# A gate and up step pair that takes the last quarter of the inner dimension two steps later

## The reference, cut to what matters

```
h = h + concatenate([oa, ob, oc, od], axis=-1) @ w_out[i]
y = _rms(h, norm_ffn_g[i])                    # y = h / sqrt(mean(h^2) + eps) * g
h = h + (silu(y @ w_gate[i]) * (y @ w_up[i])) @ w_down[i]
```

## Time and profile before

| | us |
|---|---|
| median of three runs (2075.77 to 2077.26) | 2076.1 |
| time of the profiled execution | 2075.89 |
| its span | 2074.0 |
| TensorE busy | 2054.3 (99%) |
| VectorE busy | 1533.5 (74%) |
| ScalarE busy | 1039.4 (50%) |
| mean granted clock | 0.998 |

### The profile page before, as it was taken

The page is one execution under the profiler, slowest core; times in us unless marked ns, Lnnn a source line. Parts: engine busy times, 40 slices in busy tenths (PEclk is TensorE's granted clock), DMA queues, the critical chain, the costliest instruction groups (busy, mean ns, idle before and its releaser), DMA issues.

```text
span 2074.0 us, 24910 instructions
## 1 busy us (share of the span) xinstructions
PE 2054.3 (99%) x10391; PEld 1746.8 (84%) x10391; DVE 1533.5 (74%) x1421; ACT 1039.4 (50%) x982; POOL 21.1 (1%) x40
## 2 busy tenths in 40 slices
PE   9999999999999999999999999999999999999998
PEld 8888888888888888888999987888888888888887
DVE  6576554665688888856789869978788787887565
ACT  6444444544455555545344446545455464555453
POOL 2000000000000000000000000000000000000000
PEclk9999999999999999999999999999999999999999
DMA  8655555555566655665655555746557465556462
GB/s 250 215 181 182 163 163 184 173 174 193 170 223 203 223 203 183 203 223 183 206 185 163 184 202 197 255 143 215 190 203 243 159 218 172 190 175 223 153 235 80
DMA packets 224735, 398.35 MB, mean 192 GB/s; under 512 B 11202, under 2 KB 56506, under 8 KB 224368
## 3 DMA queue, kind: packets, MB, share of 16 engines
q1 hardware_dynamic: 221344, 387.64, 56.2%
q0 software_dynamic: 2528, 8.00, 1.3%
q10 hardware_dynamic: 752, 1.12, 0.2%
HBM read 394.62 MB, written 2.12 MB: 191 GB/s over the span
## 4 chain that ended last, share of the span: by engine, by line
PE 91%; DVE 6%; ACT 1%; DMA 1%; issue 1%; ACTq 0%; SPq 0%; DVEq 0%
PE psA L679 22%; PE psA L681 21%; PE psA L680 21%; PE psA L885 6%; PE psB L679 4%; PE psB L680 4%; PE psB L681 4%; PE psA L889 3%; DVE lo L1678 2%; DVE CA L1967 1%; PE psB L943 1%; DVE raw L1695 1%; ACT hi L1216 1%; DMA X<-in_x_dram 0%; DMA raw<-in_w_up_dram 0%
## 5 line engine op out<-in xcount | busy, mean ns | idle before, releaser
L1678 DVE TENSOR_TENSOR lo<-raw,hi 128x2048 fp32r<-128x2048 f32 (+2 forms) x373 | 843.3, 2269 | 289.5 <-ACT hi L1216 287.6
L1216 ACT ACTIVATE hi<-raw 128x2048 fp32r<-128x2048 f32 (+2 forms) x373 | 706.7, 1900 | 468.6 <-PE psA L681 314.4
L679 PE MATMUL psA<-hi,XHL 128*128 128x512 f32 (+1 forms) x1048 | 409.4, 391 | 3.1 <-DVE XHL L1775 1.7
L681 PE MATMUL psA<-hi,XHL 128*128 128x512 f32 (+1 forms) x1048 | 406.5, 388 | 0.0
L680 PE MATMUL psA<-lo,XHL 128*128 128x512 f32 (+1 forms) x928 | 359.5, 387 | 0.0
L679 PE MATMUL psA<-hi,YHL 128*128 128x512 f32 x624 | 244.4, 392 | 0.0
L681 PE MATMUL psA<-hi,YHL 128*128 128x512 f32 x624 | 243.0, 389 | 0.0
L679 PEld LDWEIGHTS psA<-hi,XHL 128*128 128x128 f32 x1048 | 196.9, 188 | 44.3 <-DVE lo L1678 2.2
L681 PEld LDWEIGHTS psA<-hi,XHL 128*128 128x128 f32 x1048 | 196.7, 188 | 40.7
L680 PE MATMUL psA<-lo,YHL 128*128 128x512 f32 x576 | 224.1, 389 | 0.0
L680 PEld LDWEIGHTS psA<-lo,XHL 128*128 128x128 f32 x928 | 174.4, 188 | 34.5
(11 more groups left out here) (427 smaller groups left out, 2708.9 us busy)
## 6 DMA issues: line engine op xcount, KB each, us to landing
raw<-in_w_in_dram SPq DMA_DIRECT2D x149, 1024.0 KB, 5.1
raw<-in_w_down_dram SPq DMA_DIRECT2D x37, 1024.0 KB, 5.2
raw<-in_w_up_dram SPq DMA_DIRECT2D x35, 1024.0 KB, 5.2
raw<-in_w_gate_dram SPq DMA_DIRECT2D x35, 1024.0 KB, 5.2
raw<-in_w_out_dram SPq DMA_DIRECT2D x32, 1024.0 KB, 5.1
raw<-in_w_ple_gate_dram SPq DMA_DIRECT2D x16, 1024.0 KB, 5.1
raw<-in_w_branch_dram SPq DMA_DIRECT2D x13, 1024.0 KB, 5.1
raw in Y<-in_w_in_dram SPq DMA_DIRECT2D x9, 1024.0 KB, 5.1
```

The lines of the kernel that those rows point to most:

```text
L679: e.matmul(dst, A2[0], B2[0], start=first, stop=False, skip_group_check=True)
L681: return e.matmul(dst, A2[1], B2[0], start=False, stop=last, skip_group_check=True)
L1216: e.activation(hi[u % H][:, 0:m], raw[slot][:, 0:m], ACT.Copy).then_inc(hi_made, 1)
L1678: e.tensor_tensor(lo[slot][:, 0:m], raw[slot][:, 0:m], hi[u % H][:, 0:m].bitcast(F32), ALU.subtract).then_inc(lo_made, 1)
```

## The change: what it does

For S 0 alone the steps get another order, `START`: a, x, p2, f, e, d, p3, p0, c, g, p1. Step p3, the one that uses the last quarter of the activations in the gate product, moves from the fifth to the seventh place; e and d move up. The other ten step groups and the six of the first layer keep `STEPS`.

With it the turn of the last quarter moves by one unit, from ahead of p2 (238) to ahead of f (239), on all three engines. Its squares move on ScalarE from the end of unit 235 to the end of unit 236, behind the copy P1. The norm's root moves on VectorE from unit 239 to 241. Form e (the difference d - b, which takes b's buffer) is made behind the low part of f, where it was made ahead of that of p3. All sums of `gate_up` that stood at steps d and p0 stand at p0. Step d no longer closes quarter C; p3 does. In `fills` S 0 walks `FILLED_EARLY`, in which c comes ahead of p3.

```diff
@@ -64,6 +64,7 @@
 MIX_ORDER = (0, 3, 2, 1)
 
 STEPS = ("a", "x", "p2", "f", "p3", "e", "d", "p0", "c", "g", "p1")
+START = ("a", "x", "p2", "f", "e", "d", "p3", "p0", "c", "g", "p1")
 SOURCE = {"a": (0, 0), "b": (1, 0), "c": (0, 4), "d": (1, 4), "p0": (0, 8), "p1": (0, 12), "p2": (1, 8), "p3": (1, 12)}
 FILLED = ("a", "b", "x", "d", "p2", "f", "p3", "c", "g", "p0", "p1")
 FILLED_EARLY = ("a", "b", "x", "d", "p2", "f", "c", "p3", "g", "p0", "p1")
@@ -100,7 +101,7 @@
         group(("branch", 4 * b + f), "N", A["w_branch"][0, b], 512 * f, [[(k, 4 * b + k) for k in range(4)]])
 
     def mixed(name, W, cols, banks):
-        g = Group(len(groups), name, "S", W, cols, STEPS, len(units))
+        g = Group(len(groups), name, "S", W, cols, START if name == ("S", 0) else STEPS, len(units))
         g.banks = banks
         groups.append(g)
         for i in range(len(STEPS)):
@@ -221,8 +222,8 @@
         if g.kind == "S":
             if i:
                 continue
-            for role in FILLED_EARLY if g.name[0] == "gs" else FILLED:
-                until = u + STEPS.index("e" if role == "b" else role)
+            for role in FILLED_EARLY if g.name[0] == "gs" or g.parts == START else FILLED:
+                until = u + g.parts.index("e" if role == "b" else role)
                 if role in SOURCE:
                     n, k0 = SOURCE[role]
                     take(u, (g.name, role), until, g.W[n], k0, 4, [(g.cols[n], 512)])
@@ -457,7 +458,7 @@
             g, i = units[u]
             if g.kind != "S":
                 return places[u]
-            role = STEPS[i]
+            role = g.parts[i]
             return places[g.name, "b" if role == "e" else role]
 
         def block_of(j):
@@ -543,8 +544,8 @@
         LAST_GATES = named["gs", GATES - 1].first
         MERGE = {LAST_GATES + 3: 0, LAST_GATES + 5: 1, OUT: 2, OUT + 1: 3}
         TURN1 = {OUT + 6 + 4 * f: f for f in range(4)}
-        TURN2 = {OUT2 + 6 + 4 * f: f for f in range(4)}
         BEGIN = [named["S", j].first for j in range(11)]
+        TURN2 = {OUT2 + 6: 0, OUT2 + 10: 1, OUT2 + 14: 2, BEGIN[0] + 3: 3}
         TURN3 = {named["down", 16 + f].last + 2: f for f in range(4)}
         TURNH = {BEGIN[j + 1] + 3: j for j in (0, 2, 4, 6, 8, 9)}
         TURNH |= {named["down", 2 * j - 2].first + 1: j for j in (1, 3, 5, 7)}
@@ -801,7 +802,7 @@
 
             def mixed(u):
                 g, i = units[u]
-                role, j = STEPS[i], g.name[1]
+                role, j = g.parts[i], g.name[1]
                 early = g.name[0] == "gs"
                 free = gates_free if early else mixed_free
                 FH, FL = (GSFH, GSFL) if early else (SFH, SFL)
@@ -844,12 +845,12 @@
                     if j == 0 and not early:
                         e.wait_ge(flip_low, SECOND + 4)
                     block("D", 12, t1, last=True)
-                    x = block("C", 12, t0)
+                    x = block("C", 12, t0, last=g.parts == START)
                 elif role == "e":
                     e.wait_ge(*copied(g, "U2"))
                     x = form("A", 3)
                 elif role == "d":
-                    x = form("C", 4, last=True)
+                    x = form("C", 4, last=g.parts == STEPS)
                 elif role == "p0":
                     free(j, "B")
                     block("B", 8, t0, first=True)
@@ -1207,8 +1208,8 @@
                 g, i = units[u]
                 m = UNIT if g.kind == "S" else g.width * len(g.parts[i])
                 slot, _, landed = place(u)
-                if g.kind == "S" and STEPS[i] in FORMS:
-                    e.wait_ge(form_made, 4 * order(g) + FORMS[STEPS[i]])
+                if g.kind == "S" and g.parts[i] in FORMS:
+                    e.wait_ge(form_made, 4 * order(g) + FORMS[g.parts[i]])
                 else:
                     e.wait_ge(raw_landed[slot], landed)
                 if u >= H:
@@ -1554,7 +1555,7 @@
                 elif name == "bg":
                     e.wait_ge(bank_dve, g.freed)
                     part_high(c4(B[:, 3, :]), 1, 1.0)
-                elif name == "out2":
+                elif name == "out2" and n < 3:
                     e.wait_ge(bank_dve, g.freed)
                     squares(n, X, ss3, ss3_made)
                 elif name == "down" and n >= 16:
@@ -1593,7 +1594,7 @@
             for u in range(n_units):
                 g, i = units[u]
                 side(u)
-                if g.kind == "S" and STEPS[i] == "x":
+                if g.kind == "S" and g.parts[i] == "x":
                     mixed(u)
                 if 0 < u < n_units - AHEAD and u not in ATTEND and u not in EARLY:
                     split(u + AHEAD)
@@ -1606,10 +1607,13 @@
                 if u in ENDED and ENDED[u].name[0] == "gs":
                     first_gates(ENDED[u])
                 if g.kind == "S":
-                    if STEPS[i] != "x":
+                    if g.parts[i] != "x":
                         mixed(u)
                 elif u == g.last:
                     post(g)
+                if u == BEGIN[0]:
+                    e.wait_ge(bank_dve, freed(("out2", 3)))
+                    squares(3, X, ss3, ss3_made)
             e.wait_ge(ple_sum, 6)
             for m, (t, c, n) in enumerate(LAST):
                 ts = slice(512 * t + c, 512 * t + c + n)
@@ -1681,7 +1685,7 @@
             def mixed(u):
 
                 g, i = units[u]
-                role, j = STEPS[i], order(g)
+                role, j = g.parts[i], order(g)
                 of = {r: raw[places[g.name, r][0]][:, :] for r in FILLED}
 
                 def arrived(r):
@@ -1706,26 +1710,28 @@
                     arrived("c")
                     e.wait_ge(form_made, 4 * j + 2)
                     form("g", "c", "f")
-                elif role == "p3":
+                elif role == "p3" and g.parts == STEPS:
                     form("b", "d", "b")
                 split(u)
+                if role == "f" and g.parts == START:
+                    form("b", "d", "b")
 
             def gate_up(u):
 
                 g, i = units[u]
-                role, j = STEPS[i], g.name[1]
+                role, j = g.parts[i], g.name[1]
                 early = g.name[0] == "gs"
                 third, sums0, sums1 = (GSU3, GCG[:, 0:512], GCG[:, 512:1024]) if early else (SU3, CG1, CG2)
-                if role == "d":
+                if role == ("p0" if g.parts == START else "d"):
                     e.wait_ge(*copied(g, "U3"))
                     finish(e.tensor_tensor(sums1, sums1, third[:, :], ALU.add))
-                    e.wait_ge(unit_done, g.first + STEPS.index("p3") + 1)
+                    e.wait_ge(unit_done, g.first + g.parts.index("p3") + 1)
                     e.tensor_tensor(sums1, sums1, quarter(g, "D"), ALU.add).then_inc(gate_made, 1)
-                elif role == "p0":
-                    e.wait_ge(unit_done, g.first + STEPS.index("d") + 1)
+                if role == "p0":
+                    e.wait_ge(unit_done, g.first + max(g.parts.index("d"), g.parts.index("p3")) + 1)
                     e.wait_ge(*copied(g, "U2"))
                     e.tensor_tensor(sums0, sums0, quarter(g, "C"), ALU.add).then_inc(gate_made, 1)
-                elif role == "g" and not early:
+                if role == "g" and not early:
                     e.wait_ge(fg_tanh, j + 1)
                     e.scalar_tensor_tensor(out=CG[:, :], in0=THF[:, :], scalar=1.0, in1=CG[:, :], op0=ALU.add,
                                            op1=ALU.mult).then_inc(gate_made, 1)
@@ -2136,7 +2142,7 @@
                 if u in TURN2:
                     f = TURN2[u]
                     low(SECOND + f, XL[:, 4 * f:4 * f + 4, :], XH[:, 4 * f:4 * f + 4, :], 1, scale_cols(32, f))
-                if u == BEGIN[0] + 3:
+                if u == BEGIN[0] + 5:
                     e.wait_ge(ss3_made, 4)
                     row_sums(ss3, v2)
                     mean_eps(v2, 2048)
```

## The result

The changed kernel takes 2080.94 us (median of 15 runs, 2079.73 to 2081.95), the kernel before beside it 2076.83 (15 runs, 2075.77 to 2077.74): a ratio of 1.0021, interval 1.0014 to 1.0027, slower by 4.1 us. The profiled execution took 2081.48 us, with a span of 2079.7 against 2074.0. Three single executions of the experiments (7370.93 us in experiment 7, 2275.57 us in experiment 4, 5349.89 us of the kernel before) lie far outside all others, and the ratios leave them out.

A forecast was written before the change was run, and what follows sets the result against it. TensorE's own matmuls, 91% of the chain that ended last, were taken to bound the kernel. A stall of +2.4 us and a clock loss of +1.5 us summed to 3.9 us, giving 2080.0 us, range 2077.0 to 2082.2.

The forecast's parts named there:

- the line of 4.15 us: Whole kernel: change below 0.2% can't be told from none; chances 0.60 same, 0.37 slower, 0.03 faster.
- The early high part of f, the early copy of C, no wait ahead of p2: ScalarE makes f's high part about 1256.4, copies C at 1263.55; p2 starts right behind x at 1261.30.
- The chain to copy U2: ScalarE's copy of f's sum stands behind four pieces, the first waiting for form e; e starts about 1276.3.
- The stall's term, +2.4 us: Between f and e TensorE stands still 5.5 to 6 us, so e starts 2.4 us late against 1273.87.
- The clock's term, +1.5 us: The long stall ahead of e halves TensorE's clock; half of 2.9 us of slow matmuls is lost.
- The upper bound of 2.9 us: Largest clock loss behind the stall, if full clock is given back later than at the kernel's start.
- The root, the gate sums, the turn's place, the loads: nothing: Moved VectorE work, the moved turn and reordered weight loads were expected to add no new wait.
- the second wait: Rival, 0.10: later gate sums push VectorE past its slack in the second half-pair; about 2081.5 us.
- The stall without clock loss: Rival, 0.20: TensorE stalls ahead of e but its clock doesn't fall; 2078.5 us.
- The copy in time: Rival, 0.08: ScalarE copies right behind f, e waits about 1.1 us, starts at 1271.5; 2073.7 us.
- The useful part of the change: Up to the end of f: the step after could start at 1270.35 instead of 1273.87, gaining 3.5 us.

The follow-up runs named there:

- experiment 7: Kernel before, with only the last quarter's squares moved to the end of unit 236 on ScalarE: 2075.56 us, ratio 0.9996.
- experiment 4: Changed kernel with 22 unused matmuls between f and e, ahead of all waits of e: 2078.59 us, ratio 1.0009.
- Experiments 1: Changed kernel with ScalarE's copy U2 ahead of p3's high part instead of behind it: 2078.75 us, ratio 1.0011.
- experiment 8: Changed kernel with the last quarter's turn back at unit 238 and the root back at unit 239: 2081.38 us, ratio 1.0023.
- experiment 2: Changed kernel with copy U2 at the head of f's iteration, also ahead of the turned quarter's high part: 2076.74 us, ratio 1.0001.
- experiment 6: Changed kernel with copy U2 at the head of f's iteration and form e ahead of f's low part: 2075.54 us, ratio 0.9996.
- experiment 3: Changed kernel with 20 unused matmuls between f and e, behind the wait for e's low part: 2081.06 us, ratio 1.0020.

## Why the prediction was right, point by point

The forecast was 2080.0 us, the measured time 2080.94, inside the range. The loss is 4.1 us where 3.9 were forecast; the rest of the difference is the kernel before, which stands at 2076.83 over 15 runs against 2076.1 over three. That 3.9 lies so near to 4.1 is partly luck: of the two terms one came out 0.5 us smaller by the times and the other 0.7 us larger. And the loss lies right at the line of 4.15 us that the forecast drew between "same" (0.60) and "slower" (0.37); on which side it fell was not foreseen. With 15 runs of each kernel it is clear of the spread.

- *The early high part of f, the early copy of C, no wait ahead of p2*: right. They stand at 1256.71, 1263.82 and 1261.56, against 1256.4, 1263.55 and 1261.30 forecast, each off by the 0.26 us of the start, to 0.05 us. The turn took 1.0 us (1267.08 to 1268.08), not 0.82, which had been read right behind a stall; the 0.2 us are hidden in the stall behind f.
- *The chain to copy U2*: right in every link, to 0.15 us once the 0.26 is taken off. Form e at 1266.72 (1266.45), high e at 1269.04 (1268.77), copy at 1275.88 (1275.76), e at 1276.61 (1276.3). Experiments 1 and 2 took the copy one and two pieces forward and TensorE's stall shrank with it; experiment 8 has two of the pieces in another order, and the copy at the same place.
- *The stall's term, +2.4 us*: the profile gives 2.5 us (2.74 less the 0.26 of the start), the times 1.9 us (experiment 4 against before, interval 0 to 3.9).
- *The clock's term, +1.5 us*: right in kind, too small. By the times it is 2.2 us (4.1 less the 1.9 of experiment 4); by the profile 2.4 us, 2.2 in e's twelve matmuls and 0.2 in the first of d. The clock was low for 6.8 us in the profile, and 5.3 of them had work in them, where the start of the kernel had let me expect 2.9. So p0, forecast at 1288.6 with the clock's loss, began at 1289.9, 1.0 us later when the 0.26 is taken off. The upper bound of 2.9 us held. The reading at the start rests on the pace alone: the granted clock of 2 to 5 us reads 1.00 in the profile before, though the loads of those six matmuls take 337 ns, as they do in the low stretch of the changed kernel (0.33 us), against 0.19 otherwise.
- *The root, the gate sums, the turn's place, the loads: nothing*. Right: no wait of TensorE behind p3 is new, and experiment 8 measured turn and root. The gate sums' place was not tried alone; the next pair's p2 shows 3.0 us of slack where 2.6 were before. Of the rivals, the second wait didn't appear.
- *The stall without clock loss* is what experiment 4 made: 2078.59 us, where the rival's number was 2078.5.
- *The copy in time*: experiments 2 and 6 made it. The rival named 2073.7 us, and they gave 2076.74 and 2075.54. In experiment 2 it was too low because it left out e's own low part, ready only at about 1273.2, and the clock. In experiment 6 e's low part is early and e waits 1.18 us for the copy, as the rival had it with 1.1; but f's low part is late for that, and f waits 0.95 us, and p3 0.20. So a copy in time meets VectorE's low parts right behind it.
- *The useful part of the change*, at most 3.5 us, was a bound that no version came near. The best one is 1.3 us below the kernel before by the medians.

## What to carry to other kernels

When a step order is changed to let one input come later, look at what the moved step had covered: here it hid a copy of a running sum, and what counted was not the copy's length (0.6 us) but its place in its engine's queue (behind four pieces, 7 us from the first of them). Count the longest single stall of TensorE and not only their sum: three short ones, under 4 us together, cost the clock nothing in the profile before; one of 5.5 cost 2.2 us on top of the delay itself. If such a stall can't be avoided, matmuls of no use can buy the clock's share back: here those ahead of all waits did (experiment 4), those behind one of them didn't (experiment 3). And a part of a change can be worth more than the whole: the squares' later place alone comes out 1.0 us below the kernel before, the whole change 4.1 us above it.

## What the runs showed of the hardware

- A stall of 2.3 us (experiment 2) and one of 2.2 us (experiment 3) went with a fall of the clock to 1.2 GHz, while 1.7 us in the kernel before left it at 1.00. The forecast had taken only the long stall for dangerous. No threshold is shown by this: each is one profiled execution, and the two groups of times of experiment 3 suggest that the same stall doesn't bring the clock down every time. The fall came 1.9 us (experiment 3) to 5.0 us (experiment 8) after TensorE's last matmul ahead of the stall.
- The low stretches lasted 3.4 us (experiments 1, 2, 3 and 8) and 6.8 us in the changed kernel. In experiments 1, 2 and 8 the clock fell 0.9, 0.3 and 0.1 us after TensorE had resumed (1274.8, 1274.0 and 1277.1): a fall can come behind the stall, and then all of it lies under work.
- At the low clock the loads of 128x512 matmuls follow each other at 0.43 us against 0.227. The Trainium skill, in TensorE: Matmul & The Clock Gate, section "HAM oscillation — how this bites in real kernels", describes a kernel that waits between bursts and starts each one at half rate; this case's trace agrees, with 4.9 us for the twelve matmuls of e against 2.7. In experiments 1 and 2 it agrees only in part: e began at full pace there and slowed a little later.
